# Two transformer blocks in one fp32 program: the lead of the weight splits, joined passages, and the order of ScalarE's and VectorE's work in five stages

## The reference, cut to what matters

```python
# first block
h = rms_norm(x, g0); proj = h @ w_in
y_a = hyena(...); y_b = neighbourhood_attention(...); y_c = short_conv(...)
merged = sum(gates[i] * (y_i @ w_branch[i]))
x = x + rms_norm(merged @ w_out, g1)
h = rms_norm(x, g2)                          # "n2" in the kernel
x = x + rms_norm(cross_attention(h, rms_norm(mem), wq, wkv, wo), g3)
h = rms_norm(x, g4)                          # "n4"
x = x + rms_norm((gelu(g) * val) @ w_down, g5)   # g, val = dwconv3(h @ w_up)
# second block, with 16 meta tokens ahead
proj = rms_norm(h) @ w_in                    # "latent"
y_a = mla(6 heads); y_b = diff_attention(4 heads: p0 - lam * p1); y_c = sliding_window(6 heads)
h = h + concat(y_a, y_b, y_c) @ w_out
h = h + (silu(hn @ w_gate) * (hn @ w_up)) @ w_down
```

## Time and profile before

| what | value |
|---|---|
| median of 3 runs | 1954.23 us (1951.95 to 1955.97) |
| the profiled execution, its own time | 1953.56 us |
| its span | 1951.8 us |
| mean granted PE clock | 0.965 |
| chunks of weights, matmuls and weight loads | 289, 8987 each |
| HBM read | 165.51 MB, 87 GB/s over the span |

### The profile page before, as it was taken

The page is one execution under the profiler, slowest core; times in us unless marked ns, Lnnn a source line. Parts: engine busy times, 40 slices in busy tenths (PEclk is TensorE's granted clock), DMA queues, the critical chain, the costliest instruction groups (busy, mean ns, idle before and its releaser), DMA issues. The chain is left out here.

```text
span 1951.8 us, 22257 instructions
## 1 busy us (share of the span) xinstructions
PE 1829.9 (94%) x8987; PEld 1464.6 (75%) x8987; DVE 1011.5 (52%) x1517; ACT 733.3 (38%) x1219; POOL 289.3 (15%) x233
## 2 busy tenths in 40 slices
PE   7899999999999978989999999889878989999998
PEld 5678877788888766868888788877655768888887
DVE  6777844444444455358777522674454534444322
ACT  4433344333334433334444322444445533322221
POOL 1023500111102130141111100500100011111000
PEclk9999999999999989989999999898877989999999
DMA  5222322132224320222222222321200122222221
GB/s 185 87 86 87 106 79 76 65 121 95 97 98 164 117 75 33 76 76 87 86 97 97 87 98 87 119 81 68 88 22 32 44 75 88 97 97 97 87 97 54
DMA packets 49829, 171.13 MB, mean 88 GB/s; under 512 B 5882, under 2 KB 8570, under 8 KB 49600
## 3 DMA queue, kind: packets, MB, share of 16 engines
q1 hardware_dynamic: 45216, 155.69, 23.1%
q0 software_dynamic: 3936, 13.51, 2.0%
q10 hardware_dynamic: 576, 0.52, 0.1%
HBM read 165.51 MB, written 4.19 MB: 87 GB/s over the span
## 5 line engine op out<-in xcount | busy, mean ns | idle before, releaser
L308 DVE TENSOR_TENSOR ws_l<-raw,ws_h 128x1024 fp32r<-128x1024 f32 x289 | 387.9, 1346 | 574.3 <-ACT ws_h L300 573.9
L371 PE MATMUL ps<-h_h,ws_h 128*128 128x512 f32 (+1 forms) x1448 | 584.8, 404 | 38.9 <-DVE ws_l L308 13.3
L372 PE MATMUL ps<-h_l,ws_h 128*128 128x512 f32 (+1 forms) x1448 | 572.9, 396 | 0.0
L373 PE MATMUL ps<-h_h,ws_l 128*128 128x512 f32 (+1 forms) x1448 | 571.7, 395 | 0.0
L300 ACT ACTIVATE ws_h<-raw 128x1024 fp32r<-128x1024 f32 x289 | 303.6, 1054 | 490.4 <-PE ps L373 486.8
L371 PEld LDWEIGHTS ps<-h_h,ws_h 128*128 128x128 f32 x1448 | 278.4, 192 | 115.2 <-issue 29.1
L373 PEld LDWEIGHTS ps<-h_h,ws_l 128*128 128x128 f32 x1448 | 278.7, 192 | 62.1
L372 PEld LDWEIGHTS ps<-h_l,ws_h 128*128 128x128 f32 x1448 | 279.2, 193 | 58.4 <-issue 0.2
L371 PE MATMUL ps<-G_h,ws_h 128*128 128x512 f32 (+1 forms) x374 | 143.5, 384 | 4.2 <-DVE ws_l L308 4.2
L372 PE MATMUL ps<-G_l,ws_h 128*128 128x512 f32 (+1 forms) x374 | 143.3, 383 | 0.0
L373 PE MATMUL ps<-G_h,ws_l 128*128 128x512 f32 (+1 forms) x374 | 143.3, 383 | 0.0
(11 more groups left out here) (438 smaller groups left out, 2429.9 us busy)
## 6 DMA issues: line engine op xcount, KB each, us to landing
raw<-in_ffn_up SPq DMA_DIRECT2D x88, 512.0 KB, 3.2
raw<-in_w_merge SPq DMA_DIRECT2D x36, 512.0 KB, 3.2
raw<-in_ffn_down SPq DMA_DIRECT2D x22, 512.0 KB, 3.2
raw<-in_w_down SPq DMA_DIRECT2D x22, 512.0 KB, 3.2
raw<-in_w_hy SPq DMA_DIRECT2D x12, 512.0 KB, 4.8
raw<-in_w_sc SPq DMA_DIRECT2D x12, 512.0 KB, 3.3
raw<-in_fwd SPq DMA_DIRECT2D x8, 512.0 KB, 3.2
raw<-in_w_naqk SPq DMA_DIRECT2D x8, 512.0 KB, 3.2
```

Of the source, the lines that this page charges most:

```text
L308: dve.e.tensor_tensor(w.lo, raw[n % NRAW][:], w.hi, ALU.subtract).then_inc(*lo_made.says(("lo", n)))
L371: pe.e.matmul(o, a.hi, b.hi, start=start, stop=False, skip_group_check=True)
L372: pe.e.matmul(o, a.hi, b.lo, start=False, stop=False, skip_group_check=True)
L373: return pe.e.matmul(o, a.lo, b.hi, start=False, stop=stop, skip_group_check=True)
```

## The change

Nine edits in one:

```diff
+    lead = {"n": 2}
 def ahead(n):
-        while m < n + NSPLIT and (m < NSPLIT or over_at.get(m - NSPLIT, n + 1) <= n):
+        while m < n + lead["n"] and (m < NSPLIT or over_at.get(m - NSPLIT, n + 1) <= n):
```

Residual r1 and the query tiles (`residual_dve` is shared by all residuals, `beside` does nothing in the others):

```diff
 def residual_dve(...):
         for m in range(8):
-            beside(m)
             i, old = rings["dve T"].take(("rs", v, m))
...
                 h_rest(nv, m - 2, ngain, dst(m - 2))
+            beside(m)
...
+    XA_BESIDE = (1, 2, 3, 5)
-        residual_act("r1", ..., lambda m: chunk_act() if m in (1, 3, 5) else None)
+        residual_act("r1", ..., lambda m: chunk_act() if m in XA_BESIDE else None)
         for m in range(5):
-            f.next(8)
+            if m:
+                f.next(8)
...
+        xq_banks = Ring(place, [bank_at["k", 7], bank_at["v2", 0, 0], bank_at["v2", 0, 1], bank_at["r1", 6], bank_at["r1", 7]])
-            o = bank(("xq", t), main) if k == 0 else out_of(("xq", t))
+            o = bank(("xq", t), xq_banks) if k == 0 else out_of(("xq", t))
```

The same two lines change in `xa_dve`; tiles 3 and 4 take `xq_banks` too. Cross attention, PE and VectorE (xaD goes; Y01_FREE's "r3" names another release):

```diff
-            for kc in range(2):
-                b = bank(("xt", hd, kc), ring)
-                pe.wait_ge(("xa diag", hd))
-                for j in range(4):
-                    i = mm32(b[:, 128 * j:128 * j + 128], xaP[z][:, j, kc * 128:(kc + 1) * 128],
-                             xaD[z][:, 128 * j:128 * j + 128])
-                i.then_inc(*products.says(("done", ("xt", hd, kc)), ("xa diag used", hd)))
-                yield
+            b = [bank(("xt", hd, kc), ring) for kc in range(2)]
+            for j in range(4):
+                pe.wait_ge(("xa over", hd, j))
+                for kc in range(2):
+                    i = pe.e.transpose(b[kc][:, 128 * j:128 * j + 128], xaP[z][:, j, kc * 128:(kc + 1) * 128], ident[:])
+                if j == 3:
+                    i.then_inc(*products.says(("done", ("xt", hd)), ("xa turned", hd)))
...
+            def scaled(j):
+                dve.wait_ge(("xP", hd, j))
+                dve.e.reciprocal(s[:, 12 + j:13 + j], s[:, 8 + j:9 + j]).then_inc(*dve_part.says(("xover", hd, j)))
+                dve.wait_ge(("xover", hd, j))
+                dve.e.tensor_scalar(xaP[z][:, j, :], xaP[z][:, j, :], s[:, 12 + j:13 + j], None, ALU.mult).then_inc(
+                    *dve_part.says(("xa over", hd, j)))
...
+                if j:
+                    scaled(j - 1)
                 yield
             yield
-            dve.wait_ge(("xP", hd, 3))
-            dve.e.reciprocal(s[:, 12:16], s[:, 8:12]).then_inc(*dve_part.says(("xover", hd)))
-            dve.wait_ge(("xover", hd), ("xa diag used", hd - 2) if hd > 1 else ("off done", "r1"))
-            for j in range(4):
-                dve.e.tensor_scalar(xaD[z][:, 128 * j:128 * j + 128], ident[:], s[:, 12 + j:13 + j], None,
-                                    ALU.mult).then_inc(*dve_part.says(("xa diag", hd)))
+            scaled(3)
```

```diff
-                elif (i, j) == (2, 0):
+                elif (i, j) == (2, 1):
                     spread_tokens(v, bank(("spread", v), rings["seven"]))
...
+        down = Follow(chunk_act)
         for n in range(23):
             f.next(8 if n == 0 else 16 if n < 22 else 0)
+            if n == 22:
+                down.next(8)
...
-        f = Follow(chunk_act)
         for m in range(8):
-            f.next(22)
+            down.next(22 if m else 14)
             outputs_act("r5", m, "n4")
```

w_out_2 and the start of the second feed-forward:

```diff
-LAST_PARTS = [(m, k) for m in range(7) for k in (5, 6)] + [(m, 7) for m in range(7)] + [(7, k) for k in (5, 6, 7)]
+LAST_PARTS = [(m, k) for m in range(3) for k in (5, 6)] + [(m, 7) for m in range(3)] + [
+    (m, k) for m in range(3, 8) for k in (5, 6, 7)]
...
 def out2_act():
-        f.next(24)
-        for m in range(8):
-            if m == 7:
-                load_roots()
-            (square of x m, then h_part m; rings["f"].next(8) after m = 4)
+        f.next(8)
+        for m in range(7):
+            squared_x(m)
+            if m < 5:
+                begun(m)
+            if m in (1, 4):
+                f.next(8)
+        for m in range(5, 8):
+            begun(m)
+        rings["f"].next(8)
+        load_roots()
+        squared_x(7)
```

Attention of the second block:

```diff
-        dve.e.tensor_scalar(LAM, LAM, 0.2, None, ALU.add).then_inc(*dve_part.says("lam"))
+        dve.e.tensor_scalar(LAM, LAM, 0.2, -1.0, ALU.add, ALU.mult).then_inc(*dve_part.says("lam"))
...
-            dve.e.tensor_tensor(s, s, s0, ALU.mult).then_inc(*dve_part.says(("dif 1", u)))
-            dve.wait_ge(("dif 1", u), "lam")
-            dve.e.tensor_scalar(s, s, LAM, -1.0, ALU.mult, ALU.mult).then_inc(*dve_part.says(("dif 2", u)))
+            dve.wait_ge(("dif 0", u), "lam")
+            dve.e.scalar_tensor_tensor(s, s, LAM, s0, ALU.mult, ALU.mult).then_inc(*dve_part.says(("dif 2", u)))
...
+    def copies_first():
+        held = []
+        for step in ORDER:
+            if step[0] == "scores":
+                held.append(step)
+                continue
+            if step[0] in ("turn", "turned"):
+                n = at_unit[step[1]] + (step[0] == "turned") * len(LINE)
+                yield from (s for s in held if at_unit[s[1]] <= n)
+                held = [s for s in held if at_unit[s[1]] > n]
+            yield step
...
-        for what, u, c in ORDER:
+        for what, u, c in copies_first():
```

More of the change, by code:

```diff
@@ L1429, in program @@
     H_FREE = {"n2": ("done", ("gate in", 7, 2)), "n4": ("done", ("xq", 7)), "n6": "up 1", "n8": "w_out_2"}
-    Y01_FREE = {"r1": ("mn", 7), "r3": ("xa diag used", 3), "r5": ("off done", "r3")}
+    Y01_FREE = {"r1": ("mn", 7), "r3": ("off done", "r1"), "r5": ("off done", "r3")}
     XQ = mg
     xaT = [ya[:, 0:2, :], ya[:, 2:4, :]]
-    xaD = [y01[:, 0, :], y01[:, 1, :]]
     XA_BANKS = [(0, 1, 2), (0, 1, 2), (0, 1, 2), (4, 5, 6)]
@@ L1486, in xa_pe @@
         for m in (3, 4):
-            tile(bank(("xq", m), main), blocks, 8, hk, ("xq", m), lambda k: ("h", "n2", k))
+            tile(bank(("xq", m), xq_banks), blocks, 8, hk, ("xq", m), lambda k: ("h", "n2", k))
             if m == 3:
@@ L1522, in attend @@
             yield
-            for kc in range(2):
-                b = bank(("xt", hd, kc), ring)
-                pe.wait_ge(("xa diag", hd))
-                for j in range(4):
-                    i = mm32(b[:, 128 * j:128 * j + 128], xaP[z][:, j, kc * 128:(kc + 1) * 128],
-                             xaD[z][:, 128 * j:128 * j + 128])
-                i.then_inc(*products.says(("done", ("xt", hd, kc)), ("xa diag used", hd)))
-                yield
+            b = [bank(("xt", hd, kc), ring) for kc in range(2)]
[5 more added lines that the diff above has]
+                    i.then_inc(*products.says(("done", ("xt", hd)), ("xa turned", hd)))
+            yield
+            yield
             yield
@@ L1566, in xa_act @@
                 half_values(0)
-        residual_act("r1", "n2", "ng2", hm, chunk_act, lambda m: chunk_act() if m in (1, 3, 5) else None)
+        residual_act("r1", "n2", "ng2", hm, chunk_act, lambda m: chunk_act() if m in XA_BESIDE else None)
         half_values(1)
@@ L1592, in attend @@
                 yield
-                act.wait_ge(("xneg", hd, j), ("xa diag used", hd - 2) if hd > 1 else None)
+                act.wait_ge(("xneg", hd, j), ("xa turned", hd - 2) if hd > 1 else None)
                 act.e.activation(xaP[z][:, j, :], out_of(("xS", hd, j))[:, 0:256], ACT.Exp, bias=s[:, 4 + j:5 + j],
@@ L1602, in attend @@
             for kc in range(2):
-                act.wait_ge(("done", ("xt", hd, kc)), ("done", ("xO", hd - 2, 1)) if hd > 1 else None)
+                act.wait_ge(("done", ("xt", hd)), ("done", ("xO", hd - 2, 1)) if hd > 1 else None)
                 act.e.activation(xaT[z][:, kc, :].hi, out_of(("xt", hd, kc)), ACT.Copy).then_inc(
@@ L1649, in xa_dve @@
                 half_values(0)
-        residual_dve("r1", "ng1", "n2", "ng2", hm, chunk_dve, lambda m: chunk_dve() if m in (1, 3, 5) else None, True)
+        residual_dve("r1", "ng1", "n2", "ng2", hm, chunk_dve, lambda m: chunk_dve() if m in XA_BESIDE else None, True)
         half_values(1)
@@ L1792, in finish @@
                 *dve_part.says(("G1", i), ("gone", ("u", i, 0))))
+        down = Follow(chunk_dve)
         for n in range(23):
             f.next(8 if n == 0 else 16 if n < 22 else 0)
+            if n == 22:
+                down.next(8)
             if n == 2:
@@ L1811, in ffn1_dve @@
         rings["dve T"] = Ring(place, (0, 1, 2), ("G1", 21))
-        f = Follow(chunk_dve)
         for m in range(8):
-            f.next(22)
+            down.next(22 if m else 14)
     def ffn1_pool():
@@ L1836, in out2_act, with squared_x, begun @@
     def out2_act():
+        lead["n"] = 2
         rings["act T"] = Ring(place, (3, 4, 5), ("mix", 7))
         f = Follow(chunk_act)
-        f.next(24)
         rings["f"] = Follow(chunk_act)
-        for m in range(8):
-            if m == 7:
-                load_roots()
+        def squared_x(m):
             act.wait_ge(("x", "o2", m), *(("mix", i) for i in range(8)))
```

(25 more changed lines are left out.)

## The result

The changed kernel takes 1996.94 us in the median of 4 runs (1993.95 to 1999.27), the kernel before 1954.15 in 4. The ratio is 1.0219 (95% interval 1.0201 to 1.0236): 43 us slower, where I had forecast 8 slower, and beyond the range's upper end of 1984. Its profiled execution took 1996.81 us, with a span of 1995.0.

The account below looks back on a forecast made before the run. PE, busy 94% of the span, was taken as the bound. A loss of 52.4 us less gains of 44.3 gave +8.1, hence 1962 us predicted, range 1938 to 1984.

Parts of the forecast that it names:

- Charged 52.4: Whole kernel, lead cut to chunk n + 1: late splits cost 43.4 us plus 9.0 of clock; bounds 30 and 75.
- Merge, the first feed-forward and latent: Late splits from the shorter lead cost 11.7, 12.9 and 11.0 us in these stages, before clock charges.
- Hyena: Inverse transform: two late splits, 3.1 and 1.7 us, cost 4.8 together; five chunks at its beginning costed at nothing.
- part 5: Second block's attention: shorter lead and copies ahead of exponentials gain 23 us, 13 of gaps and 10 of clock; bounds 8, 33.
- rival (c): Attention gives only 8 us, PE waiting for P in place of PT: 1977 us in all; chance 0.22.
- The clock term: Attention, 1410 to 1490 us: granted clock rises from 0.75 to about 0.85 over 80 us, a gain of 10 us.
- The w_out_2 term: Second block's w_out: wait and slow matmuls of 6.8 us shrink, 3.4 left at the next: gain 3.5.
- r1 and query tiles: Residual ahead of the queries: PE's 8.93 us wait at 692.51 shrinks, gain 5.6 us; bounds 0 and 12.
- cross attention: Cross attention: 32 products become transposes and a 3.34 us wait shrinks, gain 5 us; bounds 0 and 8.
- ffn_down: Start of ffn_down, begun earlier: the 3.03 us wait at 1108.17 and 1.5 of clock go, net gain 3.5 us.
- rival (a): Whole kernel: one chunk ahead suffices, losses only some 10 us, so 1919 us; chance 0.08.
- rival (b): Attention gains 33 us as gaps close and the clock stays up; total gain 60.7 against 52.4, 1945 us; chance 0.24.

Follow-up runs that it names:

- experiment 3: The kernel before with only the split lead changed, to chunk n + 1 throughout: 2003.70 us, ratio 1.0276.
- experiment 1: The changed kernel with the lead put back to chunk n + 2 throughout, all other edits kept: 1933.32 us, ratio 0.9914.
- experiment 4: The kernel before with chunk n + 1 only from the second block's attention on: 1952.93 us, ratio 1.0015.
- experiment 7: The changed kernel (chunk n + 1) without ScalarE's copies ahead of exponentials in attention: 1997.98 us, ratio 1.0252 to the kernel before.
- experiment 11: The kernel before with the edits of r1, the query tiles and cross attention alone: 1949.22 us, ratio 0.9985.
- experiments 2: The changed kernel with chunk n + 2 to the latent stage's end, n + 1 from the second block's attention on: 1941.27 us, ratio 0.9956.
- experiment 9: The changed kernel (chunk n + 1) with the first feed-forward's spread back after tile (2, 0): 1989.10 us, ratio 1.0174 to the kernel before.
- experiment 12: The kernel before with the joined passage of ffn_down, w_out_2's new order and both later spreads alone: 1938.97 us, ratio 0.9920.

## Why the prediction was wrong, point by point

- **The sign and the mechanism of the loss were right.** Charged 52.4, measured 54 for the lead alone (experiment 3) and some 60 in the changed kernel (experiment 1); the intervals of the two overlap. Merge, the first feed-forward and latent each lie within 3 us of their term. The waits rose past the 55 that I named as the sign, to 78.4. That the totals agree so well is partly luck: in experiment 3 places without a term cost 7.2 (values) and 4.0 (end), and attention gave 8.2 back. Hyena didn't lose 5: VectorE's place at 159.33 came at 156.53, mostly because three subtractions ahead of it took 2.99 us where they had taken 5.21, and PE waited 1.32 there for 3.1. The row was read rightly, but its durations didn't hold. The beginning of hyena, costed at nothing, did cost nothing: PE is 4.1 us later at the chunk of 47.03 and level again at 79.35.
- **The step that failed is part 5, attention: 23 us.** It had 13 for gaps and 10 for the clock. Of the gaps, 6.5 came. Its first reason, ScalarE's splits held for a buffer, did go (four such waits before, none in the changed kernel), but the waits of PE that it was to explain stayed (experiment 4: idle 0.5 less). Its second reason, the order, holds in part. From experiment 7 to the changed kernel, which differ in it alone, the waits for copies of turned probabilities fall from 15.9 to 4.3 us over all lines, and 6 us come back in other waits: idle is 5.7 less. For the exponentials that are held back are let go at once, and other work queues behind them. ScalarE and PE in the changed kernel:

```profile
1451.28 0.61 ACT L2687 ACTIVATE P<-P,st 128x400 f32<-128x400 f32 x1
...
1451.89 0.61 ACT L2134 ACTIVATE h_h<-tmp 128x512 fp32r<-128x512 f32 x1
1453.86 0.63 ACT L2134 ACTIVATE h_h<-mo 128x512 fp32r<-128x512 f32 x1 [1.36 <-DVE mo L2870]
```

```profile
1455.26 0.79 PE L373 MATMUL ps<-h_h,ws_h 128*128 128x512 f32 x1 [2.77 <-DVE h_l L2139]
```

  The hi part at 1451.89 stands behind eight exponentials without a gap. VectorE makes its lo part before the mixed result (`mo`), so the hi part of that one (1453.86) waits 1.36, its lo part is late, and PE waits 2.77 us for it, where it waits 1.8 in experiment 7. Waits for other lo parts (L2141, 1.9 to 3.9), for `mo` (none to 1.5) and for exponentials (none to 0.9) are most of the rest. That is rival (c) in kind, with other things late. The 3.7 us for QN_l, in the result's waits, are not of this: experiment 7 has them too, and so has experiment 11, from the edits ahead of attention alone:

```profile
1302.39 0.34 PE L2542 MATMUL ps<-KN_h,QN_h 64*128 64x144 f32 x2 [3.69 <-DVE QN_l L2120]
```

  The clock term had no ground. I had the clock rise from 0.75 to 0.85 since the gaps are shorter; over the stage it fell from 0.86 to 0.82 in the changed kernel, and is 0.86 to 0.88 in the other six with the new order. The table shows it isn't tied to the idle time in the way I assumed. The 10 was also reckoned over all 80 us, in 17 of which PE stood idle; over the busy 62.66 the same rise gives 7.4.
- **Bounds left out.** The w_out_2 term (-3.5, measured +0.5) named the wait that would remain as 3.4 but didn't charge the lead again there; experiments 2 and 4 both show PE 6.6 to 6.7 later at that chunk, the second with none of the reordering, of which 4.9 and 1.5 are left over the whole row. The end (+5.1) and the memory's values (+4.1) had no term: I walked the stages with large matmul tiles and left the short chunks out, where PE takes up chunks 2.8 us apart (672.14 and 674.94 in the trace of before) or two at once (the last two), which leaves a split less than the 5.56 us that I reckoned with.
- **Other gains held.** r1 and query tiles 8.6 for 5.6, cross attention 3.3 for 5, ffn_down 4.9 for 3.5, second spread 2.6 for 2.7. The transposes are one record each, as the 32 missing instructions show.
- **The rule of double buffers** (rival (a), Trainium skill, "Trainium Kernel Development and Optimization", Best Practices) fails by measurement: with one chunk in the making the kernel before takes 2.8% longer (experiment 3), though the two split engines are busy only 52% and 38% of the time. That page speaks of DMA under compute; here the second stage is made by engines with a program of their own.
- **The range** was too narrow because attention's 8 to 33 was taken as the bounds of a gain. Nothing in the trace excluded 0: the clock term rested on one stretch of one profile. The sign given for it, attention shorter by under 10, is what came. (In rival (b), 56.1 is 3.7 more than the loss, not 3.9; nothing hangs on it.)

## What to carry to other kernels

When a buffer's lead is cut, compare for every chunk the consumer's start with the place in the producers' programs where the new, later split stands; that list was right to 3 us in each stage that it covered but hyena, and it has to include the short chunks and the last. Don't book a gain from the clock: book the idle time, and carry the clock's share as a bound of either sign. Don't judge a stage by one profile of one kernel: with the same instructions it can differ by 10 us of 250. Before crediting a reorder on an engine, ask what else of that engine's program is now behind the held work.

## What the runs showed of the hardware that was not expected

The same attention stage, with the same instructions on every engine, took 257.4 us in the changed kernel and 247.8 in experiment 9, 256.6 in the kernel before and 261.9 in experiment 11; the kernels of each pair differ only ahead of it. The idle time of PE is within 2.2 us in the first pair and 0.3 in the second. The difference is in busy time: 228.9 and 217.1 us at a mean granted clock of 0.82 and 0.87, 221.7 and 226.6 at 0.86 and 0.84.

The Trainium skill ("TensorE: Matmul & The Clock Gate", Part 1: The HAM clock gate) says that what watches PE's activity runs free of the kernel, so that the same kernel's clock differs from run to run, and puts the cost of the ramp to full clock below 1% of a typical span. The runs agree with the first: of the 21 runs of the kernel before beside experiments 1 to 4, the shortest (1943.3 us) had a mean granted clock of 0.970 over the program and the longest (1960.4) one of 0.957, and longer runs had the lower clock beside the other experiments too. The second is of one ramp, and no run here shows it by itself; in a stage with some 30 us of gaps the difference is 11.8 us of busy time in some 250, 5% of it.

Chance from run to run isn't all of it, though. Beside the same runs of the kernel before (median clock 0.965), the twelve runs of experiment 11 have a median of 0.960 and the six of experiment 12 all lie at 0.967 or above: part of it is repeated from run to run of one kernel. What in a kernel sets it stays open; filling PE's gaps in attention wasn't tried.
